# Hybrid mixer and mixture of experts on one core: tokens split into high and low parts before their norm's root is known, the root applied where the sorted rows leave PSUM, the last output chunk by token tile, router scores on 64-column tiles

## The reference, cut to what matters

```python
x = x + jnp.concatenate([y_a, y_b, y_c], axis=-1) @ w_out[l]
h = rmsnorm(x, norm2_g[l])                 # x * rsqrt(mean(x^2) + eps) * g
x = x + hierarchical_moe(h, ...)
...
pg = softmax(xt @ rg_w + rg_b)             # 4 groups
grp = argmax(pg); p_grp = pg[grp]
le = (xt @ re_w + re_b)[group grp]         # 8 experts of the group
q_top, e_top = top_k(softmax(le), 2)
gates = p_grp * q_top / sum(q_top)
expert = grp * 8 + e_top                   # 2 of 32 experts for each token
h = silu(xb @ w_gate[e]) * (xb @ w_up[e]);  y = h @ w_down[e]
```

## Time and profile before

| | us |
|---|---|
| three runs: median (lowest, highest) | 1361.91 (1360.98, 1362.93) |
| the profiled execution's own time | 1361.14 |
| its span, first to last instruction | 1359.3 |
| TensorE busy | 1235.7 (91%) |
| VectorE busy | 511.2 (38%) |
| ScalarE busy | 280.0 (21%) |
| GpSimd busy | 6.0 (0%) |
| HBM read | 469.13 MB, mean 347 GB/s |

### The profile page before, as it was taken

One profiled execution on the slowest core, in us unless ns is written; L12 is line 12 of the kernel. 1 busy time (PEld: TensorE's weight loads), 2 busy tenths in 40 slices (PEclk: granted clock), 3 DMA queues, 4 the chain that ended last, 5 costly groups with the idle time before them and its releaser, 6 DMA issues.

```text
span 1359.3 us, 16672 instructions
## 1 busy us (share of the span) xinstructions
PE 1235.7 (91%) x6468; PEld 682.4 (50%) x6468; DVE 511.2 (38%) x906; ACT 280.0 (21%) x383; POOL 6.0 (0%) x27
## 2 busy tenths in 40 slices
PE   5999999989989999989899888989898989898896
PEld 5999999978866333333333333333333333333332
DVE  5365868655437422322222222222222222222224
ACT  5443444436343100100001000000100000100002
POOL 1000000000000000000000000000000000000000
PEclk9999999989999999999999999999999999999998
DMA  8555354547466999999999999999999999999994
GB/s 274 203 181 191 128 184 155 185 155 278 148 265 245 427 427 427 429 427 428 429 429 428 429 428 429 430 427 430 428 428 429 429 428 429 428 428 429 427 423 165
DMA packets 63443, 471.80 MB, mean 347 GB/s; under 512 B 5895, under 2 KB 6407, under 8 KB 37676
## 3 DMA queue, kind: packets, MB, share of 16 engines
q1 hardware_dynamic: 63404, 471.24, 84.5%
HBM read 469.13 MB, written 2.10 MB: 347 GB/s over the span
## 4 chain that ended last, share of the span: by engine, by line
PE 55%; DMA 40%; DVE 2%; issue 2%; ACT 1%; SPq 0%; DVEq 0%; ACTq 0%
DMA ring<-in_w_up 39%; PE bank L1301 24%; PE bank L1468 15%; PE bank L1503 8%; PE bank L1516 3%; PE bank L1445 1%; PE bank L1469 1%; DMA stage<-in_w_in 1%; PE bank L1485 1%; PE bank L1411 1%; PE bank L1478 0%; DVE x_tok L1174 0%; DVE zone_u L859 0%; ACT w_hi L354 0%; PE bank L1378 0%
## 5 line engine op out<-in xcount | busy, mean ns | idle before, releaser
L1468 PE MATMUL bank<-ring,win 128*64 128x512 f32 x992 | 442.9, 600 | 64.4 <-DMA ring<-in_w_up 64.4
L1469 PE MATMUL bank<-ring,win 128*64 128x512 f32 x992 | 443.8, 601 | 0.0
L1468 PEld LDWEIGHTS bank<-ring,win 128*64 128x64 f32 x992 | 132.3, 138 | 350.4 <-issue 315.8
L1174 DVE TENSOR_TENSOR x_tok<-x_tok,bank 128x512 f32<-128x512 f32 x256 | 158.7, 682 | 264.0 <-PE bank L1516 263.1
L1503 PE MATMUL bank<-ring,hiddenT 128*64 128x512 f32 x1024 | 226.8, 594 | 18.2 <-issue 17.5
L360 DVE TENSOR_TENSOR w_lo<-stage,w_hi 128x2048 fp32r<-128x2048 f32 x60 | 137.3, 2295 | 94.5 <-ACT w_hi L354 94.2
L1301 PE MATMUL bank<-h_hi,w_hi 128*128 128x256 f32 x576 | 163.7, 284 | 1.5 <-DVE w_lo L360 1.5
L1301 PE MATMUL bank<-h_lo,w_hi 128*128 128x256 f32 x576 | 163.3, 283 | 0.0
L1301 PE MATMUL bank<-h_hi,w_lo 128*128 128x256 f32 x576 | 163.3, 283 | 0.0
L1503 PEld LDWEIGHTS bank<-ring,hiddenT 128*64 128x64 f32 x1024 | 84.4, 137 | 136.7 <-issue 115.9
L354 ACT ACTIVATE w_hi<-stage 128x2048 fp32r<-128x2048 f32 x60 | 114.8, 1917 | 144.1 <-PE bank L1301 140.2
(11 more groups left out here) (222 smaller groups left out, 839.0 us busy)
## 6 DMA issues: line engine op xcount, KB each, us to landing
ring<-in_w_gate SPq DMA_DIRECT2D x62, 2048.0 KB, 27.0
ring<-in_w_up SPq DMA_DIRECT2D x62, 2048.0 KB, 31.1
ring<-in_w_down SPq DMA_DIRECT2D x62, 2048.0 KB, 27.1
stage<-in_w_in SPq DMA_DIRECT2D x44, 1024.0 KB, 4.9
stage<-in_w_out SPq DMA_DIRECT2D x16, 1024.0 KB, 5.1
ring<-in_w_up SPq DMA_DIRECT2D x4, 1024.0 KB, 16.8
ring<-in_w_gate SPq DMA_DIRECT2D x4, 1024.0 KB, 16.5
ring<-in_w_down SPq DMA_DIRECT2D x4, 1024.0 KB, 27.9
```

The source lines that it names most:

```text
L1174: V.tensor_tensor(at, at, bank[banks[n]][:, :], ALU.add).then_inc(returned, 1)
L1468: M.matmul(bank[0][0:W_ROWS, :], rows_of[:, c, 0:W_ROWS], gate[:, at], start=(c == 0), stop=(c == C - 1))
L1469: ins = M.matmul(bank[0][UPPER, :], rows_of[:, c, 0:W_ROWS], up[:, at], start=(c == 0), stop=(c == C - 1))
```

## The change

The rows are split before the root is known. ScalarE copies each finished block of `x_tok`, unnormalised and rounded, to `x_hi` (`high_parts`, two copies of 512 elements for each block); GpSimd, idle before, subtracts to get `x_lo`, two operations for each block. For the fourth block GpSimd first writes `rstd_wide`, the roots spread over 128 columns, one tile of tokens each. The sort takes `x_hi` and `x_lo`; a product of `rstd_wide` and `pick` in plain float32 (`slot_scales`, bank 7) gives the root of each slot, ScalarE copies it to `slot_scale`, and VectorE, now alone, multiplies it and `g2` in at all sixteen evictions of each half. The sort's order is by bank: the high and low products of token tile 0 for seven banks, the slot scales, tile 1 for seven banks, and the eighth bank last.

The last chunk of the fourth output block does all of token tile 0 and then tile 1, with a count (`tile_done`) between, on which the addition of tile 0 waits. The router's scores are made on 64 columns of the array at a time, lower and upper half of a token tile, twice the number of matmuls. On VectorE the routing's copies, masks and comparisons take both token tiles in one instruction where they can; `index` keeps the two choices apart, so TensorE has twice the small products. The slots of tile 1 are read after `pick` of tile 0 is written, and the second half of `pick` is written before the evictions.

The buffers move: `x_hi` and `x_lo` take the place of `zone_u`, which is dead by then, `x_sorted` that of the projection's input; `square` writes to a scratch tile of its own and so waits for the square before.

```diff
+        with ExitStack() as early:
+            zone_u = early.enter_context(nc.sbuf_tensor("zone_u", [P, Z0 + J * ZC], F32))
+        with ExitStack() as early:
+            x_hi, x_lo = (early.enter_context(nc.sbuf_tensor(n, [P, C * S], F32R)) for n in ("x_hi", "x_lo"))
...
@@ GpSimd
+            for b in range(BLOCKS):
+                if b == BLOCKS - 1:
+                    pool.wait_ge(h_ready, T + 1)
+                    for t in range(T):
+                        pool.tensor_scalar(rstd_wide[:, t, :], ones[:, :], RSTD[:, t:t + 1], None, ALU.mult).then_inc(scale_wide, 1)
+                for t in range(T):
+                    pool.wait_ge(x_hi_made, T * b + t + 1)
+                    pool.tensor_tensor(of_block(x_lo_c, t, b), of_block(x_tok_c, t, b), of_block(x_hi_c, t, b).bitcast(F32),
+                                       ALU.subtract).then_inc(x_lo_made, 1)
...
@@ ScalarE
+            def high_parts(b):
+                for t in range(T):
+                    nc.scalar.activation(of_block(x_hi_c, t, b), of_block(x_tok_c, t, b), ACT.Copy).then_inc(x_hi_made, 1)
...
-                squares(b - 1)
-            squares(BLOCKS - 1)
+                for t in range(T):
+                    square(b - 1, t)
+                high_parts(b - 1)
+            square(BLOCKS - 1, 0)
             turned_out(BLOCKS - 1)
+            square(BLOCKS - 1, 1)
             act.wait_ge(mean_sq, 2)
             nc.scalar.activation(RT_, MS, ACT.Sqrt).then_inc(root, 1)
-            for t in range(T):
-                act.wait_ge(h_ready, T + 1)
-                act.wait_ge(used, chunk(4 * MOE_BLOCK0 - 1))
-                nc.scalar.activation(h2_hi_c[:, t], x_tok_c[:, t], ACT.Copy, scale=RSTD[:, t:t + 1]).then_inc(h2_hi_made, 1)
+            high_parts(BLOCKS - 1)
...
+            act.wait_ge(scale_made, 1)
+            nc.scalar.activation(slot_scale[:, 0:SORT], bank[7][:, 0:SORT], ACT.Copy).then_inc(scale_ready, 1)
...
@@ VectorE
             for t in range(T):
-                dve.wait_ge(h2_hi_made, t + 1)
-                V.scalar_tensor_tensor(h2_lo_c[:, t], x_tok_c[:, t], RSTD[:, t:t + 1], h2_hi_c[:, t].bitcast(F32),
-                                       ALU.mult, ALU.subtract).then_inc(h2_lo_made, 1)
+                n[t] = made_pick(t, SECOND)
...
-                    ins = V.tensor_scalar(x_sorted[:, c, at], bank[banks[i]][:, k * SORT:(k + 1) * SORT], g2[:, c:c + 1],
-                                          None, ALU.mult)
+                    ins = V.scalar_tensor_tensor(x_sorted[:, c, at], bank[banks[i]][:, k * SORT:(k + 1) * SORT], g2[:, c:c + 1],
+                                                 slot_scale[:, at], ALU.mult, ALU.mult)
...
@@ TensorE
+                    if m == by_tile:
+                        for t in range(T):
+                            for i in range(CM):
+                                ins = product(i, t)
+                            if t == 0:
+                                ins.then_inc(tile_done, 1)
...
-                        ins = M.matmul(bank[6 + t][:, 0:RW], xT[:, t, j * P:(j + 1) * P], rw[:, b * J + j, :],
-                                       start=(b == 0 and j == 0), stop=(b == BLOCKS - 1 and j == J - 1))
+                        for upper in range(2):
+                            r0 = upper * W_ROWS
+                            ins = M.matmul(bank[6 + t][r0:r0 + W_ROWS, 0:RW], xT[:, t, j * P + r0:j * P + r0 + W_ROWS],
+                                           rw[:, b * J + j, :], start=(b == 0 and j == 0), stop=(b == BLOCKS - 1 and j == J - 1))
...
+            def slot_scales(at):
+                for t in range(T):
+                    ins = M.matmul(bank[7][:, 0:SORT], rstd_wide[:, t, :], pick[:, t, at].bitcast(F32), start=(t == 0), stop=(t == T - 1))
+                ins.then_inc(scale_made, 1)
+            def sort_first(i, t):
+                for part in (x_hi_c, x_lo_c):
+                    for k in range(2):
+                        ins = sorted_from(bank[SORT_BANK[i]][:, k * SORT:(k + 1) * SORT], part, t, 2 * i + k, slice(0, SORT),
+                                          part is x_hi_c and t == 0 and k == 0, part is x_lo_c and t == T - 1 and k == 1)
+                return ins
+            pe.wait_ge(x_hi_made, T * BLOCKS)
+            pe.wait_ge(x_lo_made, T * BLOCKS)
+            pe.wait_ge(pick_ready, 1)
```

More of the change, by code:

```diff
@@ L980, in add_mixed @@
             def add_mixed(b):
-                dve.wait_ge(used, chunk(4 * (OUT_BLOCK0 + b) + 3))
                 for t in range(T):
+                    if b == BLOCKS - 1 and t == 0:
+                        dve.wait_ge(tile_done, 1)
+                    else:
+                        dve.wait_ge(used, chunk(4 * (OUT_BLOCK0 + b) + 3))
                     at = x_tok[:, t, b * NB:(b + 1) * NB]
@@ L1201, in _ @@
             hidden_made(0)
-            for i in range(0, 8, 2):
+            dve.wait_ge(scale_ready, 2)
+            for i in range(8):
                 evicted(sorted2_done, SECOND, SORT2_BANK, i, sorted2_dve)
@@ L1425, in _ @@
                     pe.wait_ge(mixed_added, T * (i - 1))
-                rows(b, b % 3, bank[2 * (i % 2):2 * (i % 2) + 2], yT_hi, yT_lo, former_block if i else layer_norm)
+                rows(b, b % 3, bank[2 * (i % 2):2 * (i % 2) + 2], yT_hi, yT_lo, former_block if i else layer_norm,
+                     STAGES - 1 if i == BLOCKS - 1 else None)
             turn_block(BLOCKS - 1)
@@ L1431, in _ @@
             pe.wait_ge(consts, ROUTE_CONSTS)
-            pe.wait_ge(index_ready, T)
+            pe.wait_ge(index_ready, 1)
             for t in range(T):
                 dst = bank[4 + t][:, 0:E]
-                later = index[:, t, 1:]
-                M.matmul(dst, before_b[:, :], later, start=True, stop=False)
-                M.matmul(dst, from_b[:, :], index[:, t, 0:E], start=False, stop=False)
-                other = index[:, 1, 0:E] if t == 0 else index[:, 0, 1:]
-                M.matmul(dst, ones_b[:, :], other, start=False, stop=True).then_inc(places_done, 1)
+                for k in range(2):
+                    M.matmul(dst, before_b[:, :], index[:, t, k, 1:], start=(k == 0), stop=False)
+                    M.matmul(dst, from_b[:, :], index[:, t, k, 0:E], start=False, stop=False)
+                    other = index[:, 1, k, 0:E] if t == 0 else index[:, 0, k, 1:]
+                    ins = M.matmul(dst, ones_b[:, :], other, start=False, stop=(k == 1))
+                ins.then_inc(places_done, 1)
             for t in range(T):
-                ins = M.matmul(bank[7][:, 0:E + 1], ones_b[:, :], index[:, t, :], start=(t == 0), stop=(t == T - 1))
+                for k in range(2):
+                    ins = M.matmul(bank[7][:, 0:E + 1], ones_b[:, :], index[:, t, k, :], start=(t == 0 and k == 0),
+                                   stop=(t == T - 1 and k == 1))
             ins.then_inc(sums_done, 1)
```

188 lines of the change are left out of this document (89 added, 99 removed).

## The result

The changed kernel takes 1362.89 us (median of 22 runs, 1360.44 to 1365.55) where the kernel before takes 1361.25 us (22 runs beside them, 1359.90 to 1363.66). The ratio is 1.0013, interval 1.0007 to 1.0019: slower by 1.0 to 2.6 us. That is inside 0.2%, but the forecast was 0.8 us faster, and the interval excludes it. Six of the 22 runs of the changed kernel stand apart, at 1364.57 to 1365.55; no other is above 1363.52, and none of the kernel before is above 1363.66. The mean of the other sixteen is 1362.5, of the kernel before 1361.3, so without the six 1.2 us of loss remain.

What follows compares the result with a forecast made beforehand. The experts' weight stream on DMA sets the end, once its 13.7 us break is over; -1.6 - 1.3 - 0.4 + 2.2 + 0.6 - 0.3 = -0.8 us gave a median of 1361.1 us, eight-in-ten range 1358.3 to 1363.0.

Steps and rivals of the forecast that it cites:

- Scores inside the projection: Three score blocks within the output projection on TensorE: 1.17 us for 1.71 each, 1.6 us saved for three.
- The tail to the scores: From the projection's last chunk to the router's logits: tile 1's logits start at about 401.5 instead of 402.85, -1.3 us.
- the six cases: The forecast of 1361.1 us (52%) and its five rivals (24, 6, 5, 7 and 6%).
- the slower one: Rival 3, slower than before: GpSimd's subtraction in steps costs far more than ScalarE's factor two; 1365.3 us at 3.5 us; 5%.
- rival 2: Router scores: 64-column products gain nothing, since the loads of a pair share a path; 1364.2 us, 6%.
- Routing and GpSimd: Logits to sort: routing saves 0.4 us; GpSimd's reading holds VectorE instructions with two SBUF inputs, +2.2 us.
- rival 3: GpSimd's subtraction in steps costs far more; the change loses from 1.8 us for one, 1365.3 us at 3.5; 5%.
- small instructions slip through: Lower bound, 0, of the 2.2 us hold of VectorE by GpSimd during routing: short VectorE instructions are not held.
- rival 1: Routing: small VectorE instructions are not held by GpSimd, the 2.2 us term goes; 1358.9 us, 24%.
- Sort: Sort on TensorE: slot scales +0.87, a wait of 0.24 goes, net +0.6 us; -0.3 us for the clock.
- What costs nothing: Early subtractions and copies, and the second sort's evictions, some 0.7 us before the first down projection: the stream does not break.
- Rival 5: The break in the DMA stream is not what counts, and the end stays: 1361.9 us, 6%.

Runs made afterwards that it cites:

- the last version: Changed kernel with GpSimd's last four operations held until pick is made, low parts sorted last, 224 bytes of padding ahead of y_hi and y_lo: 1357.05 us, ratio 0.9973.
- the late low parts: Changed kernel with 32 bytes of padding, GpSimd's last four operations held until both selection matrices are written, low parts sorted last: 1360.41 us, ratio 0.9993.

## Why the prediction was wrong

**The step that failed** is "Scores inside the projection", in what it left standing beside its own term: it put the 384 products around the score groups at no change, without a reason, and under "The tail to the scores" it took their pitch from the kernel before, 0.229 us. None of their instructions changes, but their weights move. The change gives `x_hi`, `x_lo`, `win`, `ring7` and others new places, `y_hi` and `y_lo` move by 4960 bytes, and the products run at 0.2333 us. That is +1.5 us in the profile, in a forecast of -0.8. Moving the two tiles by 32 bytes costs the kernel before 1.4 us in the products and 1.8 us in the median (ratio 1.0013). With the old start the changed kernel stands at 0.9987 (0.9978 to 0.9996). That interval holds the forecast's 0.9994, but its middle is 1 us better, most of it the sort in the profile (-0.48 where +0.3 was forecast), so it does not confirm the size of each term. None of the six cases had this term; the slower one had another mechanism.

**Scores:** right. 0.54 us a block forecast, 0.52 measured. The pairs overlap (32 in 1.06 us); rival 2 is out.

**Tail:** right. -1.3 forecast; tile 1's logits stand 3.3 us behind the projection instead of 4.68, -1.4. The scores on 64 columns alone give 0.8 of it (3.86 us in the run with nothing else); the rest comes with the order of the last chunk and of the copy, which no run takes apart.

**Routing and GpSimd:** the mechanism was right and the size a little high. -0.4 and +2.2 forecast; without holds the chain from the logits of tile 1 takes 4.63 us instead of 4.85, -0.2, and the holds cost 1.7. A subtraction in steps took 1.49 us (1.4 taken), far from the 1.8 at which rival 3 begins to lose. Of the bound "small instructions slip through" (rival 1, 24%) nothing is left: instructions of 0.2 us are held as long ones are. What I mis-sized is `rstd_wide`, 0.60 us each where I had 0.25, and the hold is not one block of 2.2 us until GpSimd's last operation: it goes instruction by instruction. Maxima, index searches and the first `masked` (0.23 us, started at 402.87) got through, while the cast of four elements, which has one input, was held; so the bound is not "two inputs from SBUF" alone. The Trainium skill (GPSIMD Engine Reference, Performance pitfalls for Q7 kernels) puts reading in steps at half as much again: 1.49 for 1.05 agrees. The run with both inputs in the same steps does not: 1.06 us each, as in sequence. The measurements decide, and the rule does not hold for every such instruction; why is open.

**Sort:** +0.6 - 0.3 forecast, +0.56 measured in the changed kernel and -0.48 with 160 bytes of padding. The four slot-scale products took 0.86 us, as forecast; the rest is when the clock rises, 6 us into the sort in the one and 4 in the other. The step that says that taking the splitting away gives no more than its 0.24 us holds for the profile it was read from, and not beyond: the old sort cannot use an early rise. Its last 16 products wait for VectorE's last low part, and where the clock rose 3.4 us into the sort (the kernel before with 32 bytes) they waited longer. TensorE's timeline there:

```profile
409.98 5.58 PE L1446 MATMUL bank<-pick,y_hi 128*128 128x256 f32 x32 [1.50 <-DVE pick L1075]
415.39 2.05 PE L1446 MATMUL bank<-pick,y_lo 128*128 128x256 f32 x16
418.48 2.16 PE L1446 MATMUL bank<-pick,y_lo 128*128 128x256 f32 x16 [1.03 <-DVE y_lo L1090]
```

So the old sort takes 10.53 to 10.67 us in all its eleven profiles, while the new one, free of VectorE, takes 10.06 to 10.21 in three and 11.04 to 11.23 in three, as the clock rises early or late. What sets the moment of the rise is open.

**What costs nothing:** right. The second sort's evictions delay the down projection of expert 0: the piece of queue behind 433.88 takes 8.55 us instead of 7.82, and the shift grows from 1.15 to 1.88. By 1286 it is back at 1.22. Rival 5 is out: what the first load gains or loses is there 860 us later, and the scores alone, and the last version, shorten the whole time by more than their intervals. One row was read loosely: the slice before the last of the earlier trace rows shows 423 GB/s, not 427 to 430, and nothing hangs on it.

**What stays open:** why the four remainders cost what they do, whether they count by themselves or against the `w` tiles, which VectorE instructions GpSimd holds and by what rule, when the clock rises in the sort, and how often a run meets the low clock in the last expert.

## What to carry to other kernels

An edit that adds or moves a tile can change the addresses of the tiles allocated behind it, and with them the pace of products that it doesn't touch (here up to 3%): compare the unchanged groups of the two traces first, and hold the addresses fixed (with padding) when an edit is to be judged by itself. Where GpSimd gets work beside a serial chain on VectorE, price it at one hold for each VectorE instruction with SBUF inputs that falls into a GpSimd instruction, up to the whole length of that instruction (an upper bound: maxima and one-element casts were not held), and move the work to a stretch in which VectorE has nothing urgent.

## What the hardware did that I had not expected

- Products of 128x128 weights and 512 columns, back to back at the full clock, take 0.2268, 0.2290, 0.2323 or 0.2334 us each, by the start of the weights' tiles modulo 256 bytes (192, 128, 64, 0), and 0.2333 at the two starts tried that are no multiple of 64 (160, 224). Over the 360 products at the full clock the ends lie 2.4 us apart, an estimate from these.
- GpSimd's subtractions held a VectorE cast of four elements (0.69 us for 0.17) and a pair of casts of two elements (1.06 us for 0.20). One-element casts and maxima in the same stretch were not held; instructions with an input in PSUM (the logits, 0.26 us) were not either.
- Fills by GpSimd, which read nothing, held VectorE as well: a pair of comparisons 0.59 us for 0.29.
- In the last expert TensorE stood still for 3.09 us in the changed kernel (up to 1318.95), and its granted clock fell to half: 8.65 us instead of 7.09 in the half that follows. The length of the wait alone does not decide it: the clock fell after waits of 1.95, 2.17 and 2.40 us in other profiles, and stayed after 1.94 us in the kernel before, 1.95 with 32 and with 64 bytes, and 2.13 with the late low parts.
